# The second and third down projection as seven block products, with the low parts of the weights made on VectorE and those of the activations on GpSimd

## The reference, cut to what matters

```python
def swiglu(x, w_gu, w_down):                     # ffn1 and ffn2 of the second block
    g, u = jnp.split(x @ w_gu, 2, axis=-1)       # w_gu: 1024 x 5632
    return (jax.nn.silu(g) * u) @ w_down         # a (1024 x 2816) @ w_down (2816 x 1024)

f = swiglu(rms_norm_2(h, ffn1_pre_g[i]), ffn1_w_gu[i], ffn1_w_down[i])
h = h + 0.5 * rms_norm_2(f, ffn1_post_g[i])
z = rms_norm_2(h, attn_pre_g[i]) @ w_in[i] + b_in[i]       # after ffn1
...
gate = jax.nn.sigmoid(rms_norm_2(h, ple_pre_g[i]) @ w_ple_gate[i])   # after ffn2
```

## Time and profile before

| | |
|---|---|
| median of three runs | 3358.51 us |
| the profiled execution | 3359.73 us |
| its span, first to last instruction | 3357.9 us |
| granted TensorE clock, mean | 0.978 |
| PE busy | 3182.2 us (95%) |
| DVE busy | 1837.1 us (55%) |
| POOL busy | 1771.7 us (53%) |
| ACT busy | 1250.6 us (37%) |
| DMA, mean | 124 GB/s |

### The profile page before, as it was taken

How to read it: one execution, slowest core, us unless ns; L and a number is a source line. 1 busy time by engine, 2 the same in 40 slices (tenths; PEclk the granted TensorE clock), 3 DMA queues, 4 the chain that set the end, 5 groups by cost and what they waited for, 6 DMA issues and landing times.

```text
span 3357.9 us, 41185 instructions
## 1 busy us (share of the span) xinstructions
PE 3182.2 (95%) x15279; PEld 2617.1 (78%) x15279; DVE 1837.1 (55%) x2613; ACT 1250.6 (37%) x2354; POOL 1771.7 (53%) x1314
## 2 busy tenths in 40 slices
PE   6978889899999999999999999989998999999998
PEld 4865578678887887888888888878877888888876
DVE  6779772799997133755541331167737655533124
ACT  4136372555453122433331231167714433322132
POOL 3331046655556777554467652344366554567653
PEclk8979899999999999999999999999999999999999
DMA  5534524323333533222335424546442323245333
GB/s 198 123 103 139 133 64 169 138 82 94 108 93 119 197 140 100 77 81 86 121 119 200 150 88 142 188 111 154 101 179 66 95 80 128 76 165 211 112 112 120
DMA packets 309011, 416.72 MB, mean 124 GB/s; under 512 B 59767, under 2 KB 231994, under 8 KB 306532
## 3 DMA queue, kind: packets, MB, share of 16 engines
q1 hardware_dynamic: 239768, 242.51, 24.3%
q10 hardware_dynamic: 64108, 154.67, 12.4%
q0 software_dynamic: 4960, 17.22, 1.6%
HBM read 326.88 MB, written 93.75 MB: 125 GB/s over the span
## 4 chain that ended last, share of the span: by engine, by line
PE 80%; DVE 9%; issue 4%; ACT 3%; POOL 2%; DMA 1%; ACTq 0%; SPq 0%; DVEq 0%; POOLq 0%
PE PS L911 71%; PE PS L2385 3%; PE PS L2402 1%; PE PS L2369 1%; PE PS L848 1%; DVE pt L781 1%; ACT act L803 1%; POOL dg_ab L2560 1%; DMA w_raw<-w_out 0%; PE PS L437 0%; DVE h_lo L905 0%; PE PS L460 0%; DVE px L784 0%; ACT gs__259 L1926 0%; DVE pr_ab L2502 0%
## 5 line engine op out<-in xcount | busy, mean ns | idle before, releaser
L1258 POOL TENSOR_TENSOR sl<-ss,sh 128x512 fp32r<-128x512 f32 x300 | 454.5, 1527 | 533.7 <-ACT sh L1249 533.7
L290 POOL TENSOR_TENSOR w_lo<-w_raw,w_hi 128x512 fp32r<-128x512 f32 x460 | 658.2, 1462 | 16.0
L286 POOL CAST w_hi<-w_raw 128x2048 fp32r<-128x2048 f32 x115 | 226.5, 1970 | 588.0 <-DMA w_raw<-w_in 195.4
L1480 DVE TENSOR_TENSOR cset<-cset,PS 128x512 f32<-128x512 f32 x360 | 235.9, 683 | 345.2 <-PE PS L911 345.1
L911 PE MATMUL PS<-h_hi,sh 128*128 128x512 f32 x960 | 374.8, 390 | 3.0 <-issue 2.5
L911 PE MATMUL PS<-h_lo,sh 128*128 128x512 f32 x960 | 374.1, 390 | 0.0
L911 PE MATMUL PS<-h_hi,sl 128*128 128x512 f32 x960 | 374.0, 390 | 0.0
L985 DVE TENSOR_TENSOR a_lo<-aT,a_hi 128x1024 fp32r<-128x1024 f32 x66 | 108.9, 1653 | 458.3 <-ACT a_hi L982 458.3
L1237 DVE TENSOR_TENSOR ss<-sr 128x512 f32<-128x512 f32 x300 | 331.0, 1104 | 0.3 <-issue 0.3
L911 PE MATMUL PS<-w_hi,a_hi 128*128 128x512 f32 x1056 | 326.3, 390 | 5.0 <-DVE a_lo L985 5.0
L911 PE MATMUL PS<-w_hi,a_lo 128*128 128x512 f32 x1056 | 325.6, 389 | 0.0
(11 more groups left out here) (356 smaller groups left out, 6496.5 us busy)
## 6 DMA issues: line engine op xcount, KB each, us to landing
w_raw<-ffn_w_down SPq DMA_DIRECT2D x88, 512.0 KB, 4.3
sr<-ffn_w_gu SPq DMA_DIRECT2D x80, 512.0 KB, 5.1
ad<-cset ACTq DMA_DIRECT2D x66, 512.0 KB, 3.1
w_raw<-w_down SPq DMA_DIRECT2D x44, 512.0 KB, 4.3
xs<-px ACTq DMA_DIRECT2D x40, 512.0 KB, 3.3
sr<-w_up SPq DMA_DIRECT2D x40, 512.0 KB, 5.1
w_raw<-w_out SPq DMA_DIRECT2D x32, 512.0 KB, 4.7
w_raw<-w_in SPq DMA_DIRECT2D x28, 512.0 KB, 5.3
```

The lines of the kernel that those rows point to most:

```text
L286: e.tensor_copy(w_hi[b][:, 0:n], w_raw[b][:, 0:n]).then_inc(S("w_hi"), 1)
L290: op = e.tensor_tensor(w_lo[b][:, s], w_raw[b][:, s], w_hi[b][:, s].bitcast(F32), ALU.subtract)
L1258: e.tensor_tensor(s.lo[p][:], src, s.hi[p][:].bitcast(F32), ALU.subtract).then_inc(S("s_op"), 1)
L1480: e.tensor_tensor(out, out, PS[:, b, :], op).then_inc(S("s_ev"), 1)
```

## The change

In passes f = 1 and 2 (p = 2 and 4) the down projection is no longer plain. Rows are split in two halves of 512, the contraction into even and odd 128-row blocks, the output columns into two halves of 512. Seven products of (512 x 1408) by (1408 x 512) are computed instead of eight. Each is 11 steps (KP) of 4 x 3 matmuls; 77 steps (NS), 924 matmuls.

**Activations.** Besides storing the result of a chunk, DVE forms five block sums or differences per pair of chunks in the up pass (`pair_even_dve`, `pair_odd_dve`, 128x512 each), and ACT stores all seven forms to DRAM tensor `sd`. In the down pass SP loads one 256 KB tile per step into a ring of six, ACT makes its high part, POOL its low part. `copies_act` now waits, before it overwrites two of the quarters of `cset`, for the pair sums and for the stores; before it waited for the store ahead of its first copy.

**Weights.** They are loaded once into SBUF (`w_rows`, where the aT of before lay) and stay. Per step DVE forms a sum or difference of two blocks (five of the seven products have one), ACT the high part, DVE the low part, in a ring of four.

**Results.** PSUM banks are used as two blocks of four; the products' results go to `yacc` in SBUF (per pass 16 copies on ACT, behind products 0, 1 and 3, and 24 adds or subtractions on DVE), and the norm reads them from there. The last product's eight adds stand in `tail_dve`.

**Streams.** The ring of the next stage is loaded one chunk ahead (at step 44) and that chunk is split by POOL at step 67; the other chunks' loads are issued after the last step.

```diff
@@ a_store_act / copies_act, f = 1, 2
+            j, odd = i // 2, i % 2
+            e.dma_start(sd[:, 1 if odd else 3, j, :], cset[odd][:, 0, odd]).then_inc(S(f"a_st{odd}"), 16)
+            e.wait_ge(S("d_sm"), 55 * (f - 1) + 5 * j + (5 if odd else 1))
+            if odd:
+                e.dma_start(sd[:, 0:7:2, j, :], st_odd[:]).then_inc(S("a_st1"), 16)
+            else:
+                e.dma_start(sd[:, 5, j, :], st_even).then_inc(S("a_st0"), 16)
...
+            if f:
+                e.wait_ge(S("f_out"), 3 + FT * f + i - 2)
+                e.activation(s[:, 1, 1], PS[:, 0, :], ACT.Copy).then_inc(S("s_ac"), 1)
+                e.wait_ge(S("s_pd"), 7 * n + 2)
+                e.activation(s[:, 1, 0], PS[:, 1, :], ACT.Copy).then_inc(S("s_ac"), 1)
+                e.wait_ge(S("d_sm"), 55 * (f - 1) + 5 * (i // 2 - 1) + 4 + i % 2)
+                if i == CL:
+                    a_store_act(e, f, 0)
+                e.wait_ge(S(f"a_st{i % 2}"), stores(f, i // 2))
+                e.activation(s[:, 0, 0], PS[:, 0, :], ACT.Copy).then_inc(S("s_ac"), 1)
+                e.wait_ge(S("s_pd"), 7 * n + 3)
+                e.activation(s[:, 0, 1], PS[:, 2, :], ACT.Copy).then_inc(S("s_ac"), 1)
+                return
@@ up_act: first of the 20 chunks
-            a_store_act(e, f, 0)
+            if not f:
+                a_store_act(e, f, 0)
             copies_act(e, f, CL)
             weight_high(e, f, 0, 5)
...
@@ up_act, last chunk, ahead of the nonlinearity
+                if i == FT - 1 and f:
+                    for s_ in range(2):
+                        seven_a_high(e, f, s_)
+                    for s_ in range(2):
+                        seven_w_high(e, f, s_)
@@ up_dve: first of the 20 chunks
                 weight_sum_dve(e, f, 0, 5)
+                pair_even_dve(e, f, 0)
+                for k in range(4):
+                    pair_odd_dve(e, f, 0, k)
                 weight_sum_dve(e, f, 0, 6)
                 turned_low_dve(e, f, 3)
@@ up_dve: after the product of gate and value
+                    if i % 2 == 0:
+                        pair_even_dve(e, f, i // 2)
+                    else:
+                        for k in range(4):
+                            if i == FT - 1 and k < 3:
+                                seven_step_dve(e, f, 3 + k)
+                            pair_odd_dve(e, f, i // 2, k)
@@ new functions
+        W_OF = (("11", "22", ALU.add), ("21", "11", ALU.subtract), ("21", "22", ALU.add), ("12", "22", ALU.subtract),
+                ("22",), ("11", "12", ALU.add), ("11",))
+        def seven_sp(e, f):
+            for s in range(NS):
+                if s < KP:
+                    seven_load_w(e, f, s)
+                seven_load_a(e, f, s)
+                if s == KP - 1:
+                    for i in range(KP, KP + 3):
+                        seven_load_w(e, f, i)
+                elif s == KP + 3:
+                    for i in range(KP + 3, KP + 5):
+                        seven_load_w(e, f, i)
+                elif s == 4 * KP:
+                    stream_load(e, G_UP[f] + CL, G_UP[f] + CL + 1)
+            if f == 2:
+                ple_sp(e)
+            step_done(e, f, NS - 1)
+        def seven_pool(e, f):
+            for s in range(NS):
+                seven_a_low(e, f, s)
+                if s == NS - 10:
+                    stream_split(e, G_UP[f] + CL, G_UP[f] + CL + 1)
+        def seven_pe(e, f):
+            for s in range(NS):
+                q, j = s // KP, s % KP
+                e.wait_ge(S("a_split"), FT + NS * F + s + 1)
+                e.wait_ge(S("s_op"), 7 * SN * (f + 1) + NS * F + s + 1)
...
+                for i in range(4):
+                    mm = three(e, [PS[:, BLOCK[BLOCK_OF[q]][i], :]], (ah[:, c], al[:, c]), [(v.w_hi[s % 4][:], v.w_lo[s % 4][:])],
+                               j == 0 and q not in (2, 5), j == KP - 1, q in (1, 2, 3, 5))
+        def seven_step_dve(e, f, s):
+            seven_w_sum(e, f, s)
+            if s > 2:
+                seven_w_low(e, f, s - 1)
+        def seven_act(e, f):
+            for s in range(2, NS):
+                if s == 6:
+                    a_store_act(e, f, FT - 1)
+                if s % KP == 3 and s // KP - 1 in (0, 1, 3):
+                    seven_copy_act(e, f, s // KP - 1)
+                if s == 20:
+                    post_load_act(e, p)
+                if 60 <= s < 64:
+                    post_sq_act(e, p, s - 60)
+                if s in (65, 67, 69, 71):
+                    post_store_act(e, p, (s - 65) // 2)
+                    norm_sq_act(e, p + 1, (s - 65) // 2)
...
+                seven_a_high(e, f, s)
+                seven_w_high(e, f, s)
+            tail_act(e, p)
+        def seven_dve(e, f):
+            for s in range(6, NS):
+                q = s // KP - 1
+                if s % KP == 4 and q in (2, 4, 5):
+                    for i in range(4):
+                        seven_sum_dve(e, f, q, i)
+                if s in (62, 64, 66, 68):
+                    post_dve(e, p, (s - 62) // 2)
...
+                seven_step_dve(e, f, s)
+            seven_w_low(e, f, NS - 1)
+            tail_dve(e, p)
@@ tail_dve
+            if p in SEVEN:
+                f = 1 + SEVEN[p]
+                seven_sum_dve(e, f, 6, 0)
+                seven_sum_dve(e, f, 6, 1)
+                post_dve(e, p, 4)
+                seven_sum_dve(e, f, 6, 2)
+                post_dve(e, p, 5)
+                seven_sum_dve(e, f, 6, 3)
...
             norm_out_dve(e, p + 1, 0)
@@ ple_pe
-            e.wait_ge(S("n_tmp"), 40)
+            e.wait_ge(S("d_ev"), 48)
@@ seven_sum_dve: for each bank i, products 4 and 6 (1 and 2 adds: product 2 and 5 have one)
+            elif q == 4:
+                e.wait_ge(S("d_ac"), 16 * F + 12 + i + 1)
+                add(i, 1, ALU.add)
+                e.wait_ge(S("d_ev"), 24 * F + i + 1)
+                add(i, 0, ALU.subtract)
```

More of the change, by code:

```diff
@@ L236, in build @@
         G_UP += [seg("up1", "pair", cols(t["ffn1_w_gu_2"]), CL)]
-        G_DN += [[seg("dn1", "rows", rows(t["ffn1_w_down_2"][0]), FT // 2) for _ in range(2)]]
         G_Z2 = seg("z2", "cols", cols(t["w_in_2"]), 9)
@@ L240, in build @@
         G_UP += [seg("up2", "pair", cols(t["ffn2_w_gu_2"]), CL)]
-        G_DN += [[seg("dn2", "rows", rows(t["ffn2_w_down_2"][0]), FT // 2) for _ in range(2)]]
         G_PLE = []
@@ L1438, in up_act @@
                 ahead(5)
-                if i == FT - 1:
+                if i == FT - 1 and not f:
                     e.wait_ge(S("a_ld0"), 16 * (f + 1))
@@ L1492, in up_dve @@
                 ahead(3)
+                if i == FT - 1 and f:
+                    for s_ in range(2):
+                        seven_w_sum(e, f, s_)
+                    for s_ in range(2):
+                        seven_w_low(e, f, s_)
                 e.wait_ge(S("s_pd"), 7 * n + 5)
@@ L1509, in up_dve @@
                 ahead(6)
+                if i == FT - 1 and f:
+                    seven_step_dve(e, f, 2)
                 if f:
@@ new lines, in pair_odd_dve @@
+        def pair_odd_dve(e, f, j, k):
+            a, b = cset[0][:, 0], cset[1][:, 0]
+            e.wait_ge(S("f_out"), 3 + FT * f + 2 * j + 1)
+            e.wait_ge(S("a_st1"), stores(f, j))
+            to, x, y, op = ((0, a[:, 0], b[:, 1], ALU.add), (2, a[:, 0], b[:, 0], ALU.add), (3, a[:, 1], b[:, 1], ALU.add),
+                            (1, b[:, 0], b[:, 1], ALU.subtract))[k]
+            e.tensor_tensor(st_odd[:, to], x, y, op).then_inc(S("d_sm"), 1)
+        KP = FT // 2
+        NS = 7 * KP
@@ new lines, in build, with __init__ @@
+        N_A = [len(range(r, NS, 5)) for r in range(5)]
+        TILE = [f"tile_ld{v}{k}" for v in range(2) for k in range(4)]
+        SUM_OF = [sum(len(W_OF[s // KP]) > 1 for s in range(k)) for k in range(NS + 1)]
+        BLOCK = ((5, 6, 7, 0), (1, 2, 3, 4))
+        BLOCK_OF = (0, 1, 1, 0, 1, 0, 1)
+        class Seven:
+            def __init__(self, f):
+                b = [R2 // KB + (G_UP[f] + i) % NBUF * 16 for i in range(2)]
+                r = R1 // KB
+                a_at = (b[1] + 12, b[0], b[0] + 4, b[1], b[1] + 4, r + 56)
+                w_at = (b[0] + 8, b[0] + 12, b[1] + 8, r + 60)
+                self.a_raw = [at(f"dar{f}{i}", [P, 512], F32, o * KB) for i, o in enumerate(a_at)]
+                self.a_lo = [at(f"dal{f}{i}", [P, 512], F32R, o * KB) for i, o in enumerate(a_at)]
+                self.a_hi = [at(f"dah{f}{i}", [P, 512], F32R, (o + 2) * KB) for i, o in enumerate(a_at)]
+                self.w_sum = [at(f"dws{f}{i}", [P, 512], F32, o * KB) for i, o in enumerate(w_at)]
+                self.w_lo = [at(f"dwl{f}{i}", [P, 512], F32R, o * KB) for i, o in enumerate(w_at)]
+                self.w_hi = [at(f"dwh{f}{i}", [P, 512], F32R, (o + 2) * KB) for i, o in enumerate(w_at)]
@@ new lines, in w_landed, with w_here, seven_load_w @@
+        def w_landed(e, f, i):
+            e.wait_ge(S(TILE[5 + i % 3]), 32 + 32 * (N_LOAD[i % 3] * (f - 1) + i // 3 + 1))
```

(43 more changed lines are left out.)

232 lines of the change are left out of this document (180 added, 52 removed).

## The result

The kernel after takes 3369.28 us (median of 8 runs, 3365.27 to 3370.53) against 3358.81 for the kernel before, a ratio of 1.0025 [1.0016, 1.0034]: slower by 8 to 10 us (5 to 11 by the interval), where I had forecast 3342 and a range up to 3364. The profiled execution took 3367.79 us.

What follows compares the result with a forecast made beforehand. PE bounds the kernel (80% of the chain of waits), by its number of matmuls. 59.9 us saved less 43.5 of stalls (starts 10.7, passes 18.8, ends 14.0) left 16.4 off 3359.73; allowing for profiling, 3342 us, range 3320 to 3364.

Steps and rivals of the forecast that it cites:

- The matmuls removed and their price: In each of two down passes 1056 matmuls become 924, at 0.2268 us each: 59.9 us off.
- the starts of the up passes: Second and third up pass: ACT's copy waits for pair sums and stores, costing 4.6 and 6.1 us.
- the clock: PE's granted clock is at its upper level and PE stays busy, so no change was priced.
- the waits of steps 57 to 68: Per down pass, DVE's adds and norm cost 3.4 us, and POOL's chunk split at step 67 costs 4.5.
- The middle products: Steps 14 to 40 of a down pass: ACT's copies and DVE's adds stay under the lead; 0, at most 2 us.
- the loads: First product of a down pass: 289 GB/s needed, one stretch moved 410, so no loss.
- Rival D: Loads set the pace of products 0 and 1, 13 us per pass, 26 more: 3368 us; chance 0.10.
- 2.5 of 2.72 us per step: Down-pass steps with a weight sum: DVE and POOL, one after the other, need 92% of the step; it fits.
- the lead of 2.9: Down pass: DVE can be at most 2.9 us ahead; work costing more at one go stalls PE.
- Rival C: DVE and POOL together bound the 55 sum steps per pass, at 3.0 us a step: 3373 us; chance 0.10.
- The ends: Ends of the second and third down pass: DVE's late tiles delay the next stage by 8.0 and 6.0 us.
- E+9.4: End of the second down pass: DVE's first low part for the next stage, counted from the last matmul's end, 8.0 us later.

Runs made afterwards that it cites:

- Run 2: Kernel after with five weight loads spread over steps 10, 12, 15, 19 and 24 instead of bunched at steps 10 and 14; 3360.77 us, 1.0006 of before.
- run 9: Kernel after with the activations' low parts made on DVE instead of POOL from step 8 of each down pass on; 3348.1 us, 0.9967 of before.
- run 7: Kernel after with POOL's subtraction cut to 8 columns, PE taking the activations' high part instead of the low; 3339.02 us, 0.9937 of before.
- run 1: Kernel after with 75 idle PE transposes added at the end of each changed down pass; 3368.98 us, 1.003 of before.

## Why the prediction was wrong

**Right.** The matmuls removed and their price; the waits that make the starts of the up passes; in place and size the waits of steps 57 to 68: 0.41, 2.59, 0.80, 2.71 and 1.17, 7.7 us against 7.9. The middle products cost nothing at steps 14 to 40. The sum for the starts, 11.4 against 10.7, is in part luck: PE's waits there grew by 8.1 us, less than forecast, and the clock behind them, which I had at nothing, made up the rest.

**The steps that failed: two terms put at nothing, the loads and the clock.** The stalls that I had priced came out at their size. What I had at 0 is the miss: from trace to trace I was off by 24.3 us, 19.9 of them inside the passes. A pass lost, by steps:

| steps | forecast | first pass | second pass |
|---|---|---|---|
| 0 to 8, the start | 1.5 | 1.2 | 0.7 |
| 9 to 13, the loads | 0 | 7.8 | 7.6 |
| 14 to 56 | 0 | 0 | 0 |
| 57 to 68 | 7.9 | 10.8 | 10.8 |

**The loads.** "One stretch moved 410 GB/s, so I take no loss" failed. The rate was there, and that is the point: from 1770 to 1784 us the DMA engines moved 385 to 402 GB/s without a pause (share 1.05), and the tiles still came late. SP stood 7.4 us waiting for the 1 MB store of the last pair, so the weights that it issued behind came late, and then the activation tiles that were issued behind the rest of 5.5 MB of weights:
```profile
1770.18 0.69 DVE L1748 TENSOR_TENSOR dws<-wr,wr 128x512 f32<-128x512 f32 x1 [4.74 <-DMA wr<-ffn_w_down]
...
1775.57 0.63 ACT L1734 ACTIVATE dah<-dar 128x512 fp32r<-128x512 f32 x1 [8.93 <-DMA dar<-sd]
```
```profile
dar<-sd SPq DMA_DIRECT2D x10, 256.0 KB, 8.5
...
sd<-st_odd ACTq DMA_DIRECT2D x1, 1024.0 KB, 7.7
```
A tile took 8.5 us to land in that stretch (1750 to 1785), where its median over the pass is 2.7. Run 2 took most of this loss away. It and the sharing, below, overlap: without GpSimd's work the waits ahead of steps 10 and 11 were 2.6 us in all instead of 4.6. Rival D had the place, with 26 us for the 15.4 measured, and I gave it 0.10.

**The clock.** "PE stays busy, so I change nothing for it" contradicted my own list of stalls. Gaps of 2.6 to 10 us were followed by 3 to 6 us at 1.2 GHz, which costs 7.7 us in the passes (4.3 and 3.3) and 15.4 over the whole more than before. Not every one was: the wait of 2.71 at 1942.51 was not. The Trainium skill (TensorE: Matmul & The Clock Gate, section Part 1: The HAM clock gate) says that idleness brings the lower clock; the trace agrees, with 1.8 us lost behind a gap of 2.79.

**What hid behind the right numbers: the pace of DVE and POOL.** I wrote 2.5 of 2.72 us per step, "it fits", and priced the stalls with the lead of 2.9. Rows of after show why that is no spare: DVE, then POOL, about steps 63 to 67.
```profile
1930.11 2.20 DVE L791 TENSOR_TENSOR px<-px,pt 128x1024 f32<-128x1024 f32 x1
1932.24 1.77 DVE L1767 TENSOR_TENSOR dwl<-dws,dwh 128x512 fp32r<-128x512 f32 x1
1933.94 1.78 DVE L1767 TENSOR_TENSOR dwl<-wr,dwh 128x512 fp32r<-128x512 f32 x1
...
1929.51 5.66 POOL L1740 TENSOR_TENSOR dal<-dar,dah 128x512 fp32r<-128x512 f32 x3 [3.18 <-ACT dah L1734]
...
1937.55 7.75 POOL L288 TENSOR_TENSOR w_lo<-w_raw,w_hi 128x512 fp32r<-128x512 f32 x4
```
The two engines go turn by turn: 1.8 for a 0.68 operation, 5.66 for three of 1.29. The shared port was known to me and in the sum for each operation by itself; what I did not see is how much hangs on it. Taken away, 31.1 of the 38.7 us lost in the passes go: all of the waits for `dwl` at 57 to 68, the clock behind them, and part of the loss at the loads. With the subtractions on DVE instead (run 9) the same steps lose 2.1 us. The Trainium skill (SBUF — State Buffer, section SBUF: two separate sides) says the loser of the pair of ports blocks for the whole instruction; run 7 agrees (L1767 with `dws`: 694 ns at most, against 1791). Rival C named this pair but as a steady slower pace from 2.72 us per step on. It came as bursts: PE waited 8 times in the first pass, not in every step. So C's mechanism is the cause of the larger part of the loss, its form isn't.

**The ends.** 21.0 against 14.0. The chain was right (first low part at E+10.45, forecast E+9.4). At the first end the rest is the clock, 3.5 of the 3.8 us by run 1. At PLE 1 of the 3.2 us is DVE's first low part, at E+10.4; transposes and matmuls ran at 0.5 there too, but run 1 won nothing back, so the rest isn't settled. The 2.7 us of each pass that lie neither in a wait nor in the clock are small change: each wait costs 0.16 us beside its length, and eight steps of the first pass took 0.13 to 0.20 longer without one.

## What to carry to other kernels

Before work is put on GpSimd beside VectorE, add both engines' operations with SBUF inputs up as if they were on one engine; if that comes near the step (92% of it here), move the work to the faster one, even if it is the busier: DVE took 69 subtractions more and got 7 us less busy. A lone stall of PE of 2.8 us cost nearly 2 us beside its length and a lone one of 1.85 nothing, so price the clock with every long stall. A load rate that fits on the average says nothing on what is queued ahead of the tile that is wanted next.
